# A decoder layer on one core: first operands of attention and of the feed-forward part loaded one stage earlier, and operands of the output projection moved to equal places modulo 512 bytes

## What is computed

```
h = rms_norm(x) @ w_in                      # 23 tiles of 128 columns: stage 1, "front"
o_a = gated linear attention(h)             # stage 1
o_b = RG-LRU branch(h)                      # stage 1
o_c = dilated attention(q, k, v of h)       # stage 2, 6 heads of 64
x2 = x + concat(o_a, o_b, o_c) @ w_out      # stage 3, "projection"
h2 = rms_norm(x2)
up = causal_conv3(h2 @ w_up)                # stage 4, "feed-forward", 22 pairs of 128 channels
out = rms_norm(x2 + (gelu(u_gate) * u_val) @ w_down)
```

## Time and profile before

| | us |
|---|---|
| median of 3 runs | 2535.85 |
| the profiled execution, its own time | 2547.3 |
| its span | 2545.5 |
| TensorE busy | 2438.4 |
| VectorE busy | 1711.6 |
| ScalarE busy | 1131.1 |
| GpSimd busy | 981.9 |

### The profile page before, as it was taken

The page is one execution under the profiler, slowest core; times in us unless marked ns, Lnnn a source line. Parts: engine busy times, 40 slices in busy tenths (PEclk is TensorE's granted clock), DMA queues, the critical chain, the costliest instruction groups (busy, mean ns, idle before and its releaser), DMA issues.

```text
span 2545.5 us, 33421 instructions
## 1 busy us (share of the span) xinstructions
PE 2438.4 (96%) x11968; PEld 1951.6 (77%) x11968; DVE 1711.6 (67%) x2324; ACT 1131.1 (44%) x2009; POOL 981.9 (39%) x784
## 2 busy tenths in 40 slices
PE   7999999999899998998699999999999999999997
PEld 5777877777677876776588888878777788787885
DVE  7554546776255676353678878767988888887655
ACT  6434254333045655321544444454664444444444
POOL 4111003432036774122455555413535656551211
PEclk9999989999899998999799999999999999999999
DMA  4333314443298523634422322378642322227764
GB/s 165 100 98 105 101 53 152 153 150 104 74 322 285 164 70 127 226 112 174 192 96 108 120 104 108 120 265 281 186 154 100 116 104 108 110 97 246 233 196 141
DMA packets 189445, 376.61 MB, mean 148 GB/s; under 512 B 17104, under 2 KB 61152, under 8 KB 180192
## 3 DMA queue, kind: packets, MB, share of 16 engines
q1 hardware_dynamic: 189280, 374.47, 43.4%
HBM read 250.43 MB, written 123.98 MB: 147 GB/s over the span
## 4 chain that ended last, share of the span: by engine, by line
PE 42%; DVE 6%; issue 1%; ACT 1%; POOL 1%; DMA 1%; SPq 0%; ACTq 0%; DVEq 0%; POOLq 0%
PE ff_bank L74 14%; PE ff_bank L76 14%; PE ff_bank L75 14%; DVE ff_y_gate L2867 2%; DVE ff_ring L2880 1%; DVE ff_ring L2828 1%; DVE ff_b_lo L2822 1%; ACT ff_y_gate L2681 0%; DMA ff_b_raw<-h_t 0%; ACT ff_e L2660 0%; DVE ff_u L2851 0%; DVE ff_u L2849 0%; DVE ff_b_raw L2813 0%; POOL ffn_rstd L2578 0%; DVE ff_y_val L2867 0%
## 5 line engine op out<-in xcount | busy, mean ns | idle before, releaser
L74 PE MATMUL ff_bank<-ff_b_hi,ff_ring 128*128 128x512 f32 x1232 | 486.3, 395 | 33.1 <-DVE ff_b_lo L2822 13.0
L76 PE MATMUL ff_bank<-ff_b_hi,ff_ring 128*128 128x512 f32 x1232 | 482.0, 391 | 0.0
L75 PE MATMUL ff_bank<-ff_b_lo,ff_ring 128*128 128x512 f32 x1232 | 481.7, 391 | 0.0
L66 PE MATMUL ip_bank<-ip_x_hi,ip_w_hi 128*128 128x512 f32 x736 | 308.9, 420 | 18.5 <-DVE ip_x_lo L708 16.2
L74 PEld LDWEIGHTS ff_bank<-ff_b_hi,ff_ring 128*128 128x128 f32 x1232 | 232.6, 189 | 97.3 <-issue 46.3
L67 PE MATMUL ip_bank<-ip_x_lo,ip_w_hi 128*128 128x512 f32 x736 | 298.7, 406 | 0.0
L68 PE MATMUL ip_bank<-ip_x_hi,ip_w_lo 128*128 128x512 f32 x736 | 297.2, 404 | 0.0
L76 PEld LDWEIGHTS ff_bank<-ff_b_hi,ff_ring 128*128 128x128 f32 x1232 | 232.6, 189 | 49.3
L75 PEld LDWEIGHTS ff_bank<-ff_b_lo,ff_ring 128*128 128x128 f32 x1232 | 232.9, 189 | 47.4 <-issue 0.2
L74 PE MATMUL ff_bank<-ff_ring 128*128 128x512 f32 x616 | 242.3, 393 | 5.4 <-DVE ff_ring L2880 5.4
L75 PE MATMUL ff_bank<-ff_ring 128*128 128x512 f32 x616 | 240.5, 390 | 0.0
(11 more groups left out here) (293 smaller groups left out, 4822.5 us busy)
## 6 DMA issues: line engine op xcount, KB each, us to landing
ff_raw<-in_slabs SPq DMA_DIRECT2D x43, 1024.0 KB, 4.8
proj_t<-ip_staged SPq DMA_DIRECT2D x92, 256.0 KB, 2.7
a_t<-ff_y_val SPq DMA_DIRECT2D x44, 512.0 KB, 2.6
t_t<-ff_t_sum SPq DMA_DIRECT2D x88, 256.0 KB, 2.0
ff_raw_ring<-t_t SPq DMA_DIRECT2D x56, 256.0 KB, 4.0
ff_raw_ring<-s_t SPq DMA_DIRECT2D x52, 256.0 KB, 3.3
rp_tables<-in_rope SPq DMA_DIRECT2D x24, 512.0 KB, 4.3
ip_w_raw<-in_w_in SPq DMA_DIRECT2D x23, 512.0 KB, 4.2
```

The source lines that it names most:

```text
L66: pe.matmul(out, w_hi[k], x_hi[k], start=(k == 0), stop=False)
L74: pe.matmul(out, w_hi, x_hi, start=first, stop=False, skip_group_check=resumed)
L75: pe.matmul(out, w_hi, x_lo, start=False, stop=False, skip_group_check=resumed)
L76: return pe.matmul(out, w_lo, x_hi, start=False, stop=last, skip_group_check=resumed)
```

## The change

The first transfers of attention and of the feed-forward part move into the stages before them, some conversions too, and the order of the first conversions in the feed-forward part is changed. The core of the diff:

```diff
 front, SP
+            def load_first_of_attention():
+                sp.wait_ge(roped, BLOCKS * (T_CV - T_CQ))
+                sp.wait_ge(lr_stored, 16 * BLOCKS)
+                wait_landed(sp, BLOCKS * (T_CV - 1))
+                sp.dma_start(idb[:, :], ident_bf).then_inc(first_in, 16)
+                sp.dma_start(mask[:, :, :], masks).then_inc(first_in, 16)
+                for a, t in ((0, T_CQ), (1, T_CK)):
+                    sp.dma_start(qk_first[:, a, :, :], proj_t[t:t + GROUPS, :, blk(0)].rearrange("g p s -> p g s")).then_inc(first_in, 16)
+                if n == BLOCKS * T_CV + 4:
+                    load_first_of_attention()
-            for p in range(2):
-                sp.wait_ge(stored[p], 16 + 16 * PROJECTS // 2)
 attention
-        mask = sb("mask", [P, 3, 2 * SPAN], BF16)
-        idb = sb("idb", [P, P], BF16)
-            sp.dma_start(idb[:, :], ident_bf).then_inc(mask_in, 16)
-            sp.dma_start(mask[:, :, :], masks).then_inc(mask_in, 16)
-            load_one(0, 0, T_CQ, qk_in)
-            load_one(0, 1, T_CK, qk_in)
             sp.dma_start(idf[:, :], ident).then_inc(consts_in, 16)
+            for p in range(2):
+                sp.wait_ge(proj_stored[p], 16 + 16 * PROJECTS // 2)
             load_one(0, 2, T_CV, values_in)
             sp.dma_start(gain[:, :], swa_gain).then_inc(gain_in, 16)
-            for b in range(1, BLOCKS):
-                load_qkv(b)
+            for b in range(BLOCKS):
+                load_one(b, 0, T_CQ, qk_in)
+                load_one(b, 1, T_CK, qk_in)
+                if b:
+                    load_one(b, 2, T_CV, values_in)
+            pool.memset(v_tok[:, :, :, :], 1.0).then_inc(ones_set, 1)
-            dve.memset(v_tok[:, :, :, :], 1.0).then_inc(cleared, 1)
-            pe.wait_ge(mask_in, 32)
-            pe.wait_ge(cleared, 2)
+            pe.wait_ge(first_in, 64)
+                            q = (qk_first if b < 4 else qkv)[heads, 0, g, b * SPAN:(b + 1) * SPAN]
 projection, places
-OP_SQUARES, OP_TOTAL, OP_MIX_EVEN, OP_W_RAW, OP_MIX_IN = 84000, 88096, 159776, 192544, 208928
+OP_SQUARES, OP_TOTAL, OP_MIX_EVEN, OP_W_RAW, OP_MIX_IN = 84480, 88576, 160256, 201216, 193024
-        mix_odd = [placed(f"mix_odd_{name}", [P, KT, NB], 92192 + 16384 * i, F32R) for i, name in enumerate(("hi", "lo"))]
+        mix_odd = [placed(f"mix_odd_{name}", [P, KT, NB], 92672 + 16384 * i, F32R) for i, name in enumerate(("hi", "lo"))]
 projection, SP
+            def load_first_of_ffn():              # called at b == 2
+                sp.wait_ge(product_done, KT * 3)
+                for o in range(7):
+                    sp.wait_ge(h_stored[o], 16)
+                for o in (B00, T1, T2, B10, T3, T4, B11):
+                    if o == T3:
+                        sp.wait_ge(x2_stored, 16 * 3)
+                        sp.wait_ge(square_ready, KT * 3)
+                    if o == B11:
+                        sp.wait_ge(mix_ready, KT * BLOCKS)
+                    sp.dma_start(h_raw[:, o, :, :], h_t[o]).then_inc(h_in[o], 16)
+            def load_first_slabs():               # called at b == 1, after load_mix(3)
+                sp.wait_ge(w_ready, OUT_SLABS)
+                for g in range(2):
+                    sp.dma_start(slab[:, g, :, :], slabs[g]).then_inc(slab_in[g], 16)
-            sp.wait_ge(stored, 16 * BLOCKS)
-            for o in range(7):
-                sp.wait_ge(h_stored[o], 16)
 projection, ACT (after square k == 3 of block 3), DVE (after addition m == 4), POOL (before n == 28)
+                act.wait_ge(h_in[B00], 16)
+                for i in range(KH):
+                    act.activation(h_hi[:, i, :], h_raw[:, B00, i, :], ACT.Copy).then_inc(h_hi_ready, 1)
+                act.wait_ge(slab_in[0], 16)
+                act.activation(slot[:, 0, :], slab[:, 0, 0, :], ACT.Copy).then_inc(h_hi_ready, 1)
+            # DVE: the low parts of the same five; POOL: the three sums of slab 0
+                for k in range(KT if b + 1 < BLOCKS else KT - 1):
-            root(BLOCKS - 1)
-            dve.wait_ge(rstd_ready, BLOCKS)
-            sum_squares(BLOCKS - 1)
 feed-forward
-            # SP: the loads of slab 0, slab 1 and the seven h_t
+            sp.wait_ge(x2_stored, 16 * BLOCKS)    # SP, after the loads of conv and gains
+            # ACT
+                    act.sem_inc(b_hi_ready, KH)
+                    act.sem_inc(w_hi_ready, 1)
+                    for i in range(1, 7):
+                        high_w(0, i)
+                        if i == 6:
+                            high_w(0, 7)
                         for k in range(KH):
                             high_b(0, KH * i + k)
-                        if i:
-                            high_w(0, i)
+                        if i in (1, 3, 5):
+                            keep(0, 0, i // 2)
                     act.wait_ge(consts_ready, 2)
                     act.wait_ge(consts_in, 16)
-                    keep(0, 0, 0)
-                    keep(0, 0, 1)
-                    high_w(0, 7)
                     high_w(0, 8)
+                    root_of_projection()
+            # PE, after the first product
+                        pe.matmul(banks[3][:, :], ones[:, :], op_total[:, 1, :], start=True, stop=False)
+                        pe.matmul(banks[3][:, :], ones[:, :], op_squares[:, 1, :], start=False, stop=True).then_inc(op_sum_done, 1)
```

218 lines of the change are left out of this document (121 added, 97 removed).

## The result

The median went from 2542.5 us (7 runs of the kernel before, beside the changed one) to 2515.8 us (7 runs, 2502.8 to 2524.3): a ratio of 0.9911 with an interval of 0.9887 to 0.9934. The forecast was 2494, its range 2488 to 2506. The forecast of 2494 is off by 21.8 us; 6.7 of these are no error of the terms: it was counted from 2535.85, the median of three runs, and seven runs gave 2542.5. The profiled execution took 2519.7 us (span 2517.9).

The account below looks back on a forecast made before the run. TensorE, busy 96% of the span, was taken as the bound, so savings lie in its waits or matmul pitch. Terms summed 10.0 + 5.0 + 28.3 - 1.6 = 41.7 us; 2535.85 - 41.7 = 2494 us, range 2488 to 2506.

Parts of the forecast that it names:

- Term 3: From the projection's last product to dense feed-forward work: the 35th matmul starts at 1216.7, gaining 28.3 us (24 to 30.5).
- and from there TensorE is dense: Feed-forward: from its 35th matmul on TensorE runs without waits, as before the change; a ScalarE slip costs up to 2 us.
- The check of ScalarE in the forecast: Feed-forward start: an operand with weights takes ScalarE 2.75 us against TensorE's 2.72; no stall, margin 0.2 us.
- ScalarE's order and GpSimd: Rival, feed-forward start: slips there, with VectorE and GpSimd excluding each other, bring back some 6 us; 2500 us, chance 0.10.
- Term 1: Attention start: the last store's landing leaves the front, so TensorE turns the values at 696.5, gaining 10.0 us (6.5 to 11.7).
- what is late next are the values: Attention start: after q and k, the values are the next late load, issued at about 691.7 and landing at 696.2.
- Term 2: Projection: equal places of weights and mix cut the pitch from 0.2333 to 0.2267 us; 744 matmuls gain 5.0 us, all on the path.
- Term 4: Attention: operand places become 256 apart, costing 1.6 us over 480 turns and 240 products (nothing to 4.8 us).
- Places do nothing: Rival, projection and attention: the 0.2333 pitch has another cause, so terms 2 and 4 vanish; 2497.5 us, chance 0.08.
- The wait changes its name to the values: Rival, attention start: TensorE waits for values instead of q and k, so term 1 is 6.5 us; 2497.5 us, chance 0.05.
- The projection pays for the `h_t` loads: Rival, projection: x of block 3 shares the queue with `h_t` loads, costing 8 us, at worst 15; 2502 or 2509, chance 0.10.
- the slower case: Rival, attention: weight loads at places half of 512 apart no longer overlap, costing 104 us; 2597 us, chance 0.03.

Follow-up runs that it names:

- all, all moves: "moves" with the first pair's last VectorE move right behind its third and ScalarE's copy of the second pair's second product ahead of gelu; 2504.1 us, ratio 0.985.
- all: "starts, lows" with GpSimd's last two down-weight sums behind staging of tiles 16, 17, slab 0's last sum first, seventh weight operand ahead of T4's parts; 2504.6 us, 0.987.
- places alone: Kernel before with only the projection's weights placed 32 bytes further, at the mix's place modulo 512; 2536.3 us, ratio 0.999.
- starts, lows: Changed kernel with attention loads reordered, ninth weight operand and ScalarE's copies reordered, slab 1 sums held to the sixth operand, projection's low parts early; 2510.0 us, ratio 0.988.
- gap: "all" with VectorE waiting for GpSimd's first sum of slab 1 ahead of the eighth weight operand's low part; 2506.6 us, ratio 0.987.
- moves, gap: "gap" with VectorE's first two moves of the first pair out of PSUM ahead of the eighth weight operand's low part; 2505.9 us, ratio 0.985.
- moves: "all" with VectorE's first two moves of the first pair out of PSUM ahead of the eighth weight operand's low part; 2509.8 us, ratio 0.987.

## Why the prediction was wrong

**Term 3, start of the feed-forward: 28.3 us predicted, 16.2 and 17.9 kept.** The first part of it was right: first matmul 3.23 us behind the projection's last (3.6 predicted), the 35th at 12.8 us behind it in place of 44.0. That is 2.8 us better than the 15.6 forecast, and partly luck: the forecast had 2.2 us for a fall of the clock, and in this profile there was none; in the second one there was, and the 35th came at 14.4. The step that failed is "and from there TensorE is dense", with its slip of at most 2 us. It measured one engine's start and took it for the stage's. In the kernel before TensorE came last; the other engines had used its 8.65 and 13.0 us of waiting to get ahead. What I had to ask is when VectorE is through. Its first conversion of the stage moved from 14.8 to 3.7 us behind the projection's last matmul, 11.1 us; five conversions moved into the projection, at 0.6 us another 3.0; and it lost a wait of 4.5 us for ScalarE, which was itself held by TensorE. Together 18.6 us, an estimate of what this change could gain with VectorE's work as it stood. Up to the first gelu it was 17.8 us (60.2 to 42.4) and 18.4 in the second profile, and at the 385th matmul 16.2 and 17.9. So some ten of the 28.3 us were not to be had by starting earlier alone; seven came back by other orders of work, below. The check of ScalarE in the forecast (2.75 us against 2.72) was made only up to S3, and no such sum was made for VectorE; nor did the sum put a price on VectorE and GpSimd working side by side, though the row of 10.09 us was there and a rival named it.

The rival that named this, ScalarE's order and GpSimd, had the mechanism and 6 us for it. It said slips add up; but slips could be mended, and TensorE's waits moved from the 97th to the 133rd to the 217th matmul as each was. With these mended, and slab 2 and GpSimd's sums moved, the 385th is at 101.2 us, 7 us earlier than in the first profile (5 against the second). A TensorE dense from the 35th on would have been there at 12.8 + 350 x 0.2267 = 92.2 us. The 9 us between can be read from the trace of "all, all moves": 1.6 ahead of the 35th matmul (14.4 us), where the clock was at half for 3.4 us; 5.5 at the two waits for copies of ScalarE, the 157th and 217th matmul; 1.7 in a second stretch at half clock, also of 3.4 us. What sets those two copies was not taken apart.

**Term 1, start of the attention: 10.0 predicted, 10.3 for the start, and 1 to 10 us of it lost again at tile 4.** Start and values came as worked out (values 0.39 us late). The step that failed is "what is late next are the values". Before, the q, k and v loads had 8.3 us of TensorE's waiting as a head start on the first tile; this is the cover that the change took away. Their 9 MB and all that stands behind them in the queue now end later with respect to the tiles, and the first store of sums, on the same queue, lands at 32 us, where the third tile's copy wants it at 27 to 30. The prediction counted the issues up to the values and none behind them. Two other orders of the loads only moved the loss, since the chain of down-weight sums then comes late (5.8 us; 7.0 and 6.7 in two kernels with the other order); taking that chain's end off the path as well cures it (0.1 in "all", 0.0 to 0.7 in the five kernels built on it). The first profile with its 10.6 us is the extreme; six others with the same order of loads lost 1.2 to 2.0, and took 308.8 to 311.2 us for the attention, where the attention as it was before took 306.7 to 309.3 in four profiles.

**Term 2, pitch in the projection: 5.0 predicted.** The pitch is as forecast, 0.2267 in place of 0.2333 us, and it is the places that do it, which "places alone" shows. What failed is "all on the path": VectorE, with the norms and combinations in the third block, does not get faster, so 1.4 to 2.0 us return as a longer wait ahead of the fourth block. The stage gained 2.4 us in both comparisons of first profiles (0.6 with the second profile of the changed kernel, where a wait for VectorE's additions in the first block was 4.0 us, 2.6 in the kernel before). Nine profiles of the changed kernel's projection took 184.3 to 188.9 us, so the gain of one pair is uncertain by 2 us. Ordering VectorE's work took away the wait at the fourth block; the stage then took 182.0 to 185.2 in seven profiles.

**Term 4, places in the attention: 1.6 us lost predicted, nothing measured.** The weight loads of the turns, before and after (ns min/median/max):

```profile
L1729 PEld LDWEIGHTS at_t<-at_idf,at_probs x480: 137/141/217, 708.9 to 996.0; 128*128 128x128 f32 x160
```

```profile
L1736 PEld LDWEIGHTS at_t<-at_idf,at_probs x480: 137/141/333, 688.7 to 986.5; 128*128 128x128 f32 x160
```

From start to next start these matmuls lie 109 ns apart (median) in both kernels, and so do the pairs with the masks, and tiles from the 27th on take 7.61 us in both. The step that failed is the scaling of 6.7 ns at 512 columns to short matmuls. The Trainium skill (SBUF — State Buffer, the section on the two sides) says that TensorE never waits on anyone; these rows agree, the 6.7 ns of the projection do not, and there the measurement decides.

**The rivals.** Places do nothing: refuted in the projection. The wait changes its name to the values: 0.4 us. The projection pays for the `h_t` loads: no wait for x of block 3. No weight load stopped overlapping, so the slower case is refuted. Added up from the stages of the first pair of profiles: 10.3 - 9.5 + 2.4 + 16.2 - 0.4 = 19.0 us, and the front's clock gives 8.6 more, which is chance: 27.6 of span. With the second profile of the changed kernel: 10.3 - 3.1 + 0.6 + 17.9 - 0.4 = 25.3, and 6.1 from the front. The medians' 25 to 27 us agree with the latter's stages.

**A better version.** "All, all moves", picked from several close ones, is at 0.9851 (0.9829 to 0.9873) of the kernel before; the changed kernel was at 0.9899 (0.9879 to 0.9919) in its second set of runs. The two sets were not run side by side; their intervals are just apart: some 0.5%, 12 us, faster than the changed kernel.

## What to carry to other kernels

A wait of the critical engine is a head start for all others. Before a wait is booked as gain, add up for each other engine and each queue what it must get done until the next meeting point, from its own start and not from TensorE's; the gain is that of the slowest of these sums. If waits move from one instruction to the next as each is taken away and a later marker stays put, look at the engine that is busy nine tenths of the stretch: here 2.8 us less of its busy time, with GpSimd no longer held off, brought the first gelu 2.3 us and the 385th matmul 1.1 us earlier, where the four reorderings after "all" had moved neither forward.

## What the runs showed of the hardware that I had not expected

VectorE can keep GpSimd out for many instructions, not one. A GpSimd addition of 1.3 us took 10.1 us (kernel before), 10.7 ("starts, lows"), 7.6 ("all") and 4.0 ("gap") while VectorE had subtraction after subtraction ready, 15, 16 and 11 of them in the first three, and got in when VectorE first stood still. In "moves, gap", "moves" and "all, all moves" it took 4.0 us, and its last 1.3 us begin with VectorE's first move out of PSUM, which reads only one operand from SBUF. Once in, both alternate, VectorE at 1.78 us each in place of 0.68, GpSimd at 1.7. At other times (changed kernel, 1200.52) it got in at once; what decides that isn't shown. The Trainium skill (SBUF — State Buffer, the two sides) says that whichever of the two starts first holds the shared ports for that instruction; the alternation agrees, and the hold-off over ten and more instructions goes beyond it.

In the projection a weight operand at another place modulo 512 than the moving operand costs 5 to 9 ns of a 512-column matmul (232 to 236 ns against 227), whether 32, 128 or 256 bytes apart, and beside such a one the matmuls at equal places took 1 to 2 ns more. In the attention, with 128 columns and 256 bytes apart, nothing could be measured (109 ns).
